# The last quarter of the output: GpSimd's queue adds scaled blocks onto a residual already in DRAM

## The reference, cut to what matters

```
ff = jnp.square(jax.nn.relu(h @ mlp_w1[l])) @ mlp_w2[l]
x = x + rmsnorm(ff, norm_post_mlp[l])
```

## Time and profile before

| | us |
|---|---|
| median of three runs | 2417.36 |
| the profiled execution, its own time | 2418.61 |
| its span | 2416.8 |
| PE busy in the span | 2389.3 |
| DVE busy in the span | 1685.4 |
| POOL busy in the span | 1288.2 |
| ACT busy in the span | 806.5 |

### The profile page before, as it was taken

How to read it: one execution, slowest core, us unless ns; L and a number is a source line. 1 busy time by engine, 2 the same in 40 slices (tenths; PEclk the granted TensorE clock), 3 DMA queues, 4 the chain that set the end, 5 groups by cost and what they waited for, 6 DMA issues and landing times.

```text
span 2416.8 us, 31435 instructions
## 1 busy us (share of the span) xinstructions
PE 2389.3 (99%) x11806; PEld 1967.4 (81%) x11806; DVE 1685.4 (70%) x1818; ACT 806.5 (33%) x1181; POOL 1288.2 (53%) x956
## 2 busy tenths in 40 slices
PE   8999999999999999999999999999999999999998
PEld 6788888888788888888878888888887888888887
DVE  6889889888988788879865537652895444444464
ACT  3443432455122222221122214253444434243422
POOL 0877774333322223223667766745667666656564
PEclk9999999999999999999999999999999999999999
DMA  7323323111211111124864445422532212131253
GB/s 282 115 88 113 123 113 131 61 61 59 80 44 43 43 43 43 43 87 142 268 215 142 147 140 165 176 95 70 175 130 70 96 59 98 57 100 53 85 177 122
DMA packets 91385, 263.28 MB, mean 109 GB/s; under 512 B 8464, under 2 KB 11792, under 8 KB 90256
## 3 DMA queue, kind: packets, MB, share of 16 engines
q1 hardware_dynamic: 75728, 227.26, 27.4%
q10 hardware_dynamic: 15552, 34.61, 4.1%
HBM read 214.64 MB, written 47.19 MB: 108 GB/s over the span
## 4 chain that ended last, share of the span: by engine, by line
PE 92%; DVE 4%; issue 1%; POOL 1%; ACT 1%; DMA 0%; ACTq 0%; SPq 0%; DVEq 0%; POOLq 0%
PE ps L519 25%; PE ps L521 24%; PE ps L520 24%; PE xb L519 2%; PE xb L521 2%; PE xb L520 2%; PE xa L519 2%; PE xa L521 2%; PE xa L520 2%; PE ps L573 1%; PE xb L720 1%; PE xb L749 1%; PE xb L752 1%; PE xa L740 1%; DVE h_lo L1087 1%
## 5 line engine op out<-in xcount | busy, mean ns | idle before, releaser
L2695 POOL TENSOR_TENSOR small<-small 128x1 f32<-128x1 f32 x176 | 53.9, 306 | 789.4 <-PE ps L521 612.0
L2698 POOL TENSOR_TENSOR w_lo<-w_raw,w_hi 128x1024 fp32r<-128x1024 f32 x176 | 454.9, 2584 | 14.7
L519 PE MATMUL ps<-h_hi,w_hi 128*128 128x512 f32 x928 | 368.3, 397 | 0.2 <-DVE hg_zc L1507 0.2
L521 PE MATMUL ps<-h_hi,w_lo 128*128 128x512 f32 x928 | 362.0, 390 | 0.0
L520 PE MATMUL ps<-h_lo,w_hi 128*128 128x512 f32 x928 | 361.7, 390 | 0.0
L2789 POOL TENSOR_TENSOR m_lo<-m_raw,m_hi 128x512 fp32r<-128x512 f32 x144 | 197.2, 1383 | 145.2 <-ACT m_hi L2096 144.4
L519 PE MATMUL ps<-yb_hi,w_hi 128*128 128x512 f32 x608 | 238.7, 393 | 0.0
L521 PE MATMUL ps<-yb_hi,w_lo 128*128 128x512 f32 x608 | 236.6, 389 | 0.0
L520 PE MATMUL ps<-yb_lo,w_hi 128*128 128x512 f32 x608 | 236.6, 389 | 0.0
L519 PEld LDWEIGHTS ps<-h_hi,w_hi 128*128 128x128 f32 x928 | 174.2, 188 | 37.8 <-issue 1.2
L521 PEld LDWEIGHTS ps<-h_hi,w_lo 128*128 128x128 f32 x928 | 174.2, 188 | 37.0
(11 more groups left out here) (416 smaller groups left out, 5613.6 us busy)
## 6 DMA issues: line engine op xcount, KB each, us to landing
w_raw<-wall SPq DMA_DIRECT2D x226, 512.0 KB, 3.5
m_raw<-wall SPq DMA_DIRECT2D x96, 256.0 KB, 2.7
gst<-gate_d SPq DMA_DIRECT2D x24, 512.0 KB, 4.8
w_kv<-wall SPq DMA_DIRECT2D x16, 512.0 KB, 4.8
x_d<-xx ACTq DMA_DIRECT2D x16, 512.0 KB, 3.7
raw_odd<-wall SPq DMA_DIRECT2D x14, 512.0 KB, 4.1
x_sb<-xT SPq DMA_DIRECT2D x2, 2048.0 KB, 15.6
kv_d<-kv SPq DMA_DIRECT2D x4, 1024.0 KB, 7.3
```

Source lines behind the costliest of these rows:

```text
L519: nc.tensor.matmul(out, wh, xh, start=start, stop=False, skip_group_check=onto)
L521: return nc.tensor.matmul(out, wl, xh, start=False, stop=stop, skip_group_check=onto)
L2695: nc.gpsimd.tensor_tensor(small[:, 13:14], small[:, 12:13], small[:, 12:13], ALU.add)
L2698: nc.gpsimd.tensor_tensor(w_lo[:, u], w_raw[:, u], w_hi[:, u].bitcast(F32), ALU.subtract).then_inc(w_split, 1)
```

## The change

For the last quarter of the tokens (q = 1), the residual is put into `out` beforehand: ACT's queue copies these 256 columns of `x_d` to `out`, from DRAM to DRAM, right behind the four loads of `xs_end`. VectorE then makes only one instruction for a pair, the product with `rn[1]` and -1. GpSimd's queue issues the four stores, with an accumulating DMA: it adds the 256 KB of `xx[1]` onto what lies in `out`. It waits once for the copy (`base_in`) and for each pair for `x_new`. SP's queue stores q = 0 as before, and at the end waits for both kinds of stores. Two semaphores are used a second time, which moves no instruction.

```
+        def end_rows(d, j, q):
+            rows = d[2 * j * P:(2 * j + 2) * P, HALF + q * QUARTER:HALF + (q + 1) * QUARTER]
+            return rows.rearrange("(t p) n -> p t n", p=P)
...
                 if q:
                     dve.wait_ge(y_gained, GAINED_OLD + 2 * j + 2)
                     rows = rn[1][:, cols].rearrange("p (o n) -> p o n", o=1).to_broadcast([P, 2, QUARTER])
-                    done(mul(pair, pair, rows))
-                else:
-                    for t in (2 * j, 2 * j + 1):
...
+                    v.scalar_tensor_tensor(pair, pair, -1.0, rows, ALU.mult, ALU.mult).then_inc(x_new, 1)
+                    return
+                for t in (2 * j, 2 * j + 1):
...
                 sub(pair, xs_end[:, j, :, cols], pair).then_inc(x_new, 1)
...
             for j in range(4):
                 load_residual(5, j)
+            act.dma_start(out[:, HALF + QUARTER:], x_d[:, HALF + QUARTER:]).then_inc(base_in, 16)
...
+            pool.wait_ge(base_in, BASE_OLD + 16)
+            for j in range(4):
+                pool.wait_ge(x_new, 4 * 6 + j + 1)
+                nc.gpsimd.dma_start(end_rows(out, j, 1), xx[1][:, 2 * j:2 * j + 2, quarter(1)], accum_op=ALU.add).then_inc(end_added, 16)
...
-            for q in range(2):
-                for j in range(4):
-                    sp.wait_ge(x_new, 4 * (5 + q) + j + 1)
-                    rows = out[2 * j * P:(2 * j + 2) * P, HALF + q * QUARTER:HALF + (q + 1) * QUARTER]
-                    sp.dma_start(rows.rearrange("(t p) n -> p t n", p=P), xx[1][:, 2 * j:2 * j + 2, quarter(q)]).then_inc(out_stored, 16)
-            sp.wait_ge(out_stored, 16 * 12)
+            for j in range(4):
+                sp.wait_ge(x_new, 4 * 5 + j + 1)
+                sp.dma_start(end_rows(out, j, 0), xx[1][:, 2 * j:2 * j + 2, quarter(0)]).then_inc(out_stored, 16)
+            sp.wait_ge(out_stored, 16 * 8)
+            sp.wait_ge(end_added, 16 * 4)
```

More of the change, by code:

```diff
@@ L457, in build @@
         kv_hi_done, keys_stored, kv_stored, up_relued = sem("kv_hi_done"), sem("keys_stored"), sem("kv_stored"), sem("up_relued")
-        xsq_done, xacc_done, x_stat, x_rt = sem("xsq_done"), sem("xacc_done"), sem("x_stat"), sem("x_rt")
+        xsq_done, xacc_done, end_added, x_rt = sem("xsq_done"), sem("xacc_done"), sem("end_added"), sem("x_rt")
         h_normed, h_hi_done, h_split = sem("h_normed"), sem("h_hi_done"), sem("h_split")
@@ L496, in build @@
         y_gained, GAINED_OLD = mem_rt, 1
+        base_in, BASE_OLD = mem_normed, 1
         SUM_OLD, BLOCK_OLD, PART_OLD, UP_OLD = 4 * SEVENS, 7 * SEVENS, 3 * SEVENS, 16 * (SEVENS - SEVENS // 2)
@@ L598, in _ @@
                 mm = nc.tensor.matmul(xb[:, cols], ones[:].bitcast(F32), x_acc[:, cols], start=True, stop=True)
-            mm.then_inc(x_stat, 1)
+            mm.then_inc(mem_stat, 1)
             for n in range(KB + 1, 2 * KB):
@@ L1933, in quarter_residual @@
                     rows = rn[1][:, cols].rearrange("p (o n) -> p o n", o=1).to_broadcast([P, 2, QUARTER])
-                    done(mul(pair, pair, rows))
-                else:
-                    for t in (2 * j, 2 * j + 1):
-                        last = s.at(scaled(xx[1][:, t, cols], xx[1][:, t, cols], par[:, t, G_POST_MLP:G_POST_MLP + 1], rn[1][:, cols]))
+                    v.scalar_tensor_tensor(pair, pair, -1.0, rows, ALU.mult, ALU.mult).then_inc(x_new, 1)
+                    return
+                for t in (2 * j, 2 * j + 1):
+                    last = s.at(scaled(xx[1][:, t, cols], xx[1][:, t, cols], par[:, t, G_POST_MLP:G_POST_MLP + 1], rn[1][:, cols]))
                     s.wait(last)
@@ L2127, in values_high @@
                     a.activation(kv_sb[2][:, mt, cols], ps[mt][:, cols], ACT.Identity, scale=m_rt[:, mt:mt + 1]).then_inc(kv_hi_done, 1)
-            act.wait_ge(x_stat, 1)
+            act.wait_ge(mem_stat, 2)
             rsqrt(x_r[:], x_acc[:], xb[:], 1.0 / D).then_inc(x_rt, 1)
```

## The result

| | before | after |
|---|---|---|
| time, median of 12 runs each (lowest to highest) | 2418.43 us (2417.26 to 2420.12) | 2423.38 us (2421.17 to 2426.58) |
| ratio, 95% interval | | 1.0022 (1.0013 to 1.0030) |
| profiled execution: own time, span | 2418.61, 2416.8 us | 2423.64, 2421.8 us |
| granted clock of PE, mean | 0.998 | 0.996 |

The change costs 4.95 us, 0.205%. Forecast were 2419.6 us in a range of 2415.6 to 2425.2 and a cost of 2.2 us. The time is in the range; the cost is more than twice the forecast's, and stands right on the bound of 0.2% that the text drew. Of the 3.8 us between 2419.6 and 2423.38, 1.1 are in the starting point: the forecast began at 2417.36, the median of three runs, and that of twelve is 2418.43. The time around the span is unchanged: 1.84 us after, 1.81 before.

The account below looks back on a forecast made before the run. The prediction took PE, busy for 99% of the span, to bound the kernel. It added 1.6 us for the tail and 0.6 for the copy, 2.2 us later than the median 2417.36: 2419.6 us, range 2415.6 to 2425.2.

Parts of the forecast that it names:

- What bounds the kernel, and the two places: PE, busy 99% of the span; time can change only where PE would wait or behind its last matmul.
- VectorE's side of the tail: Behind the root: four subtractions and their waits go, so the last product ends 2.9 us before the last subtraction did.
- The stores' side: Kernel's end: four adding stores on GpSimd's queue set it, so the span ends at 2418.45, 1.6 us later than before.
- L: Kernel's end, from the fourth store's issue to its landing: taken as 2.9 us, between 2.1 and 4.8.
- G: Kernel's end, GpSimd's time per DMA issue: taken as 1.4 us, between 0.37 and 2.40.
- The rival of GpSimd's issue: Behind the root: slow issues bind, cost above 4.8 us from 2.0 us each; 2423.7 at 2.4; chance 0.30 including first call.
- A first call: Rival at GpSimd's first DMA: fetching its code delays the queue, past the bound from 3.2 us; chance 0.06.
- The copy in the block: Last block: the copy delays weight loads that GpSimd waits for; PE loses 0.6 us, between nothing and 2.7.
- hidden parts: Last block: the copy's issue on ACT's queue, behind the residual loads, delays nothing, as ACT is idle for 5.29 us.
- exposed load: Last block: weight load issued near 2370.4 takes about 5.6 us instead of 3.2, costing PE 0.3 us.
- sign of being wrong: At PE's end: the prediction called itself wrong if that end moved by more than 3 us.
- The sum: Whole kernel: 1.6 us at the end plus 0.6 in the last block, 2.2 us later; chance of same 0.67.

Follow-up runs that it names:

- e2: Changed kernel without the copy: four products behind the root, plain stores by SP's queue, residual missing in the last quarter; 2417.29 us, ratio 0.9991.
- e1: Kernel before (subtractions kept, no copy), with the four last plain stores moved from SP's queue to GpSimd's; 2419.18 us, ratio 1.0001.
- e6: Changed kernel with two adding DMAs of 512 KB in place of four of 256 KB; 2425.74 us (one run).
- e9: Changed kernel with copy and adding DMA for the first pair only, the others subtracted and stored by SP as before; 2417.54 us, ratio 0.9993.
- e5: Changed kernel plus one plain 64 KB DMA to a scratch tensor, issued by GpSimd some 20 us ahead of the end; 2424.02 us, ratio 1.0018.
- e3: Changed kernel with plain stores in place of adding ones, still from GpSimd's queue and with the copy; 2420.87 us, ratio 1.0004.
- e10: Changed kernel with the copy issued later, behind ACT's squares of q = 0, when all weights are in; 2422.28 us, ratio 1.0011.
- e7: Changed kernel with adding DMAs of half the width, as many pieces of 512 B instead of 1 KB; 2421.25 us (one run).
- e8: Kernel before, with GpSimd doing the last pair's product and subtraction, VectorE the other three interleaved; 2420.38 us, ratio 1.0008.
- e4: Kernel before plus the copy alone, the last quarter subtracted on VectorE and stored by SP's queue after it; 2421.92 us, ratio 1.0011.
- after_again: The changed kernel measured once more, unaltered, beside the kernel before; 2424.52 us, ratio 1.0022.

## Why the prediction was right or wrong

**What bounds the kernel, and the two places.** Right. All that the change cost lies in the tail and in the last block.

**VectorE's side of the tail, -2.9 us.** The instructions came as worked out: 0.61 us apart, 0.69 each, the last done 2.53 us after the root (2.56 forecast). Worth is 2.34 (e2), because stores that follow each other at 0.61 us queue on engines that need 0.78. The profile of before had that number, and I had used it only for the adding stores.

**The stores' side.** This is the step that failed, and by the size of one term. Counted from the root's end, forecast against measured:

| | forecast | changed kernel |
|---|---|---|
| first product done | 0.73 | 0.72 |
| until GpSimd starts its first issue | 0 | 0.67 |
| four issues | 4 x 1.4 = 5.6 | 5.10 |
| L, from the last issue to landing | 2.9 | 5.1 |
| close | 0.4 | 0.4 |
| sum | 9.6 | 12.0 |

The bounds for G held (0.73 plain, 1.24 adding, between 0.37 and 2.40), and the middle was close. L = 2.9 was too low by 2.2 us, even past its upper bound of 4.8. It rested on the engines' part being twice that of a plain store, 1.56 us a store, "about the same pace" as G. It is 2.0: 118 ns a packet against 46, 2.6 times. With that the engines are slower than GpSimd, a queue grows on them from the first store on, and L, which I had taken as one store's latency, holds the whole of it. The slower of two paces sets the end; I had put them at 1.4 and 1.56, called them equal, and followed the one that turned out the faster. Beside that, 0.67 us pass between a product's end and GpSimd's issue, for which the sum had nothing; SP's queue starts within 0.1 us. In e1, behind a subtraction, GpSimd took 0.3; what makes the difference is open.

The Trainium skill (Collectives: The Full Stack, "The bandwidth ceiling: the fold count and why AG ≠ RS ≠ AR") says half the rate of a copy for a DMA that adds. By that, as an estimate, an adding packet takes twice the plain 46 ns, 92 ns; measured are 113 to 122 at 1 KB (after, e6, e9), so the direction agrees and the size does not.

**The rival of GpSimd's issue.** It named the right place and sign, but not the mechanism: G stayed at 1.24, far below its turning point of 2.0, and e6 shows that the end doesn't follow it. The chance of 0.30 for slower had its mass on the wrong engine. **A first call**: 0.2 to 0.8 us of tail, 0.15 of it in the first issue (1.37 us, 1.23 in e5).

**The copy in the block, +0.6 us within 0 to 2.7.** Its hidden parts were right: the issue takes 0.62 us on ACT's queue, and nothing waits for it. The exposed load was forecast to take 5.6 us instead of 3.2; it took 4.5 in the first profile (4.5 to 6.3 in the seven with the whole copy). The comparison with 3.2 flatters the copy's part, since without any copy the same load takes anything from 3.2 to 4.6 us (4.5 in e1, 4.6 in e2). POOL's timeline of the first profile shows two waits, against the one of 1.44 us in the earlier trace rows:

```profile
2371.73 0.19 POOL L2702 TENSOR_TENSOR small<-small 128x1 f32<-128x1 f32 x1 [0.59 <-DMA w_raw<-wall]
...
2375.97 1.05 POOL L2847 TENSOR_SCALAR keep_hi<-w_raw 128x1024 fp32r<-128x1024 f32 x1 [0.56 <-DMA w_raw<-wall]
```

Together they are 1.15 us, less than the 1.44, because the load before had landed after 7.2 us and not 8.0: this execution was a lucky one, and its block lost nothing. And the DMA engines show the extra traffic where it was expected, with the share at 1.04 and 0.76 from 2368 to 2376 us, in place of 0.78 and 0.25:

```profile
2368.00:2372.00 4.00, 4.00 (x20) 3.20 (x18) 0.70 (x2) 0.60 (x1) 3.33 (x4) 1.00 1.04 389
2372.00:2376.00 4.00, 4.00 (x19) 3.34 (x18) 0.18 (x1) 0.63 (x1) 3.36 (x3) 1.00 0.76 284
```

The size was too low: the middle of seven profiles is 2.3 us, and two, 3.7 (e3) and 4.3 (e5), are beyond the upper end of 2.7 and beyond the 3 us that the prediction named as a sign of being wrong. "Whatever delays a weight load beyond that stops PE, for good" was the right rule. But GpSimd did not work "without a pause" to the end, as the row at 2386.11 shows: its last load had no slack left towards GpSimd. What the sum lacked is this, that the shifted chain can meet something else that it had missed before by luck, and that nothing later gives slack back.

**The sum, +2.2 us.** By the runs: tail +4.0 to +4.3, block 0 to 4.3, by time 1.6 to 2 (4.95 and 5.35 less e10's 3.40, with overlapping intervals), minus what scatter there is; measured 4.95 and 5.35. That the first pair of profiles also differs by 5.0 us is chance: there 4.0 are the tail and 0.95 the scatter ahead of the last block. Both terms were low, and in both it was the DMA engines: their work for an adding packet, and what they do to loads when something is added beside them. The forecast of "within 0.2%" missed by a hair (0.205 and 0.22%), the 2.2 us by more than as much again; the range held because it was wide, up to 7.8 us above the median that it started from, and not because its terms were right.

## What to carry to other kernels

A DMA that adds is no free addition: work out the busy time of the DMA engines for it, with some 2.6 times the plain packet's at 1 KB (118 ns against 46 here), and compare that with the pace of its issues before taking either as the bound. An instruction on VectorE behind the last dependence is worth only what the stores' engines can follow, and it takes little (0.78 us a store against 0.61) for them not to. In a kernel in which one engine is never idle, look for the chain with the least slack to it before adding traffic, and take several profiles, since one of them may lose nothing.

## What the runs showed that I had not expected

An adding DMA's packet costs 118 ns at 1 KB and 80 at 512 B, and GpSimd 1.24 us an issue of 256 KB whatever the bytes (e7), where a plain one costs 0.73 (e1, e3). A plain DMA from GpSimd's queue goes in 320 packets to the megabyte, an adding one in 1088 (e3).

VectorE is slowed on this kind of two-operand instruction by a factor of up to 2.5 while GpSimd runs one too (0.69 to 1.74 us, e8).

And PE's clock: in two of the five profiles with a wait of about 2 us, PE came out of it at a lower granted clock. The windows of e5, with PE busy for 0.27 of the 2 us ahead of it:

```profile
2390.00:2392.00 2.00, 0.27 (x2) 0.27 (x3) 0.28 (x1) 0.39 (x1) 2.00 (x2) 1.00 0.00 0
2392.00:2394.00 2.00, 2.00 (x12) 2.00 (x12) 0.00 (x0) 0.00 (x0) 0.40 (x1) 0.56 0.09 33
2394.00:2396.00 2.00, 2.00 (x13) 2.00 (x12) 0.00 (x0) 0.00 (x0) 0.00 (x0) 0.58 0.00 0
2396.00:2398.00 2.00, 2.00 (x20) 2.00 (x19) 0.76 (x2) 0.42 (x1) 0.00 (x0) 1.00 0.00 0
```

In the 4 us behind the wait the column PEclk is at 0.56 and 0.58, near the lower of the two levels (1.2 GHz), and PE gets 12 and 13 matmuls done in 2 us instead of 20; then it is at 1.00 (2.4 GHz) again. That is about 15 matmuls, or 1.5 us, on top of the wait, and e3 shows the same (0.67 and 0.50). Without it the two longest blocks, 52.15 and 51.56, would be near the 49.93 to 50.28 of the other three. The waits were 2.46 us in e5 and 2.05 in e3. In e4, e6 and after_again, with waits of 2.05, 2.18 and 1.71 us, the clock stayed at 1.00; what tells the one from the other is left open.
